# Query and key projections of the prompt rows as three fp32r products of split weights and split x, and the convolution state loaded later

## What is computed

```python
q, k, v, z, xbc, dt = jnp.split(x @ w_in, IN_SPLITS, axis=-1)
q = _rope(q.reshape(b, L, 2 * ATT_HEADS, ATT_QK_DIM), pos)
k = _rope(k.reshape(b, L, 2 * ATT_HEADS, ATT_QK_DIM), pos)
...
xbc_pad = jnp.concatenate([conv_prev.astype(xbc.dtype), xbc], axis=1)
conv = conv_b + sum(xbc_pad[:, i:i + L] * conv_w[i] for i in range(CONV_WIDTH))
```

## Time and profile before

| | us |
|---|---|
| median of 3 runs | 1794.18 |
| lowest, highest | 1792.43, 1798.73 |
| profiled execution, span | 1790.7 |

### The profile page before, as it was taken

One profiled execution on the slowest core, in us unless ns is written; L12 is line 12 of the kernel. 1 busy time (PEld: TensorE's weight loads), 2 busy tenths in 40 slices (PEclk: granted clock), 3 DMA queues, 4 the chain that ended last, 5 costly groups with the idle time before them and its releaser, 6 DMA issues.

```text
span 1790.7 us, 23663 instructions
## 1 busy us (share of the span) xinstructions
PE 1743.2 (97%) x8760; PEld 1362.3 (76%) x8760; DVE 1214.5 (68%) x1659; ACT 845.4 (47%) x898; POOL 111.8 (6%) x120
## 2 busy tenths in 40 slices
PE   7999999999999999999999999999999999999998
PEld 4646487689999574558677888888888888888886
DVE  2687635255544287552715989899898989898994
ACT  1122211144442122212204777777777777777774
POOL 0630000000000252000001000000000000000000
PEclk9999999999999999999998999999999999999999
DMA  9556554855424445663672989899998989898980
GB/s 321 189 201 213 217 188 153 287 171 188 166 94 178 156 162 199 218 229 135 242 258 72 349 298 381 335 380 338 372 394 315 392 318 387 320 384 336 379 321 26
DMA packets 218514, 459.32 MB, mean 257 GB/s; under 512 B 10878, under 2 KB 49976, under 8 KB 218422
## 3 DMA queue, kind: packets, MB, share of 16 engines
q1 hardware_dynamic: 212710, 442.63, 68.3%
q0 software_dynamic: 3424, 11.50, 2.0%
q10 hardware_dynamic: 2304, 4.20, 0.6%
HBM read 444.97 MB, written 13.46 MB: 256 GB/s over the span
## 4 chain that ended last, share of the span: by engine, by line
PE 85%; DVE 7%; ACT 4%; issue 1%; DMA 1%; SPq 1%; POOL 0%; ACTq 0%; DVEq 0%; POOLq 0%
PE bank L1228 83%; PE bank L1232 3%; DVE arena L2701 1%; DVE ring_low L2170 1%; ACT high L1784 1%; DMA out<-mem_rows 1%; DVE R L2315 1%; ACT L1784 1%; ACT arena L1855 0%; POOL arena L972 0%; ACT ye_high L1823 0%; ACT SQ L1876 0%; DVE st L2673 0%; DVE st L2594 0%; SPq L734 0%
## 5 line engine op out<-in xcount | busy, mean ns | idle before, releaser
L2170 DVE TENSOR_TENSOR ring_low<-ring,high 128x2048 fp32r<-128x2048 f32 x264 | 598.7, 2288 | 81.3 <-ACT high L1784 80.5
L1784 ACT ACTIVATE high<-ring 128x2048 fp32r<-128x2048 f32 x264 | 505.1, 1918 | 141.8 <-PE bank L1228 137.6
L1228 PE MATMUL bank<-high,xg_high 128*128 128x512 f32 x704 | 278.1, 395 | 7.3 <-DVE ring_low L2170 7.0
L1228 PE MATMUL bank<-ring_low,xg_high 128*128 128x512 f32 x704 | 274.6, 390 | 0.0
L1228 PE MATMUL bank<-high,xg_low 128*128 128x512 f32 x704 | 274.2, 389 | 0.0
L1228 PEld LDWEIGHTS bank<-high,xg_high 128*128 128x128 f32 x704 | 132.2, 188 | 34.7 <-DVE ring_low L2170 8.4
L1228 PEld LDWEIGHTS bank<-ring_low,xg_high 128*128 128x128 f32 x704 | 132.2, 188 | 28.0
L1228 PEld LDWEIGHTS bank<-high,xg_low 128*128 128x128 f32 x704 | 132.3, 188 | 25.7
L1855 ACT ACTIVATE arena<-bank 128x512 f32<-128x512 f32 (+3 forms) x95 | 46.3, 525 | 217.1 <-PE bank L1228 141.5
L1228 PE MATMUL bank<-high,he_high 128*128 128x512 f32 x352 | 140.0, 398 | 0.0
L1228 PE MATMUL bank<-ring_low,he_high 128*128 128x512 f32 x352 | 137.4, 390 | 0.0
(11 more groups left out here) (327 smaller groups left out, 2578.0 us busy)
## 6 DMA issues: line engine op xcount, KB each, us to landing
ring<-in_w_exp_gu SPq DMA_DIRECT2D x176, 1024.0 KB, 9.9
ring<-in_w_exp_down SPq DMA_DIRECT2D x40, 2048.0 KB, 10.5
ring<-in_w_in SPq DMA_DIRECT2D x12, 2048.0 KB, 11.2
ring<-in_w_ffn_gu SPq DMA_DIRECT2D x22, 1024.0 KB, 8.7
ring<-in_w_ckv SPq DMA_DIRECT2D x8, 2048.0 KB, 9.1
ring<-in_cache_mem_k SPq DMA_DIRECT2D x16, 1024.0 KB, 8.1
ring<-in_cache_mem_v SPq DMA_DIRECT2D x16, 1024.0 KB, 6.6
ring<-in_cache_attn_k SPq DMA_DIRECT2D x32, 256.0 KB, 3.9
```

The costliest lines, as they stand in the source:

```text
L1228: return M.matmul(out, lhsT, rhs, start=start, stop=stop)
L1784: S.activation(high_bufs[h % HIGH_BUFS][:], ring[:, s, j * HALF:(j + 1) * HALF], ACT.Copy).then_inc(split_high, 1)
L2170: V.tensor_tensor(ring_low[:, s, part], ring[:, s, part], high_bufs[h % HIGH_BUFS][:], ALU.subtract).then_inc(split_low, 1)
```

## The change

The q and k products of the prompt rows (t = 0 and 1) are no longer fp32 products of `xT` and `ring`. They become three fp32r products for each of the eight chunks: `xq_high` by high weights, `xq_low` by high weights, `xq_high` by low weights.

- ACT writes `xq_high` (8 x 128 x 264, in SQ's memory) and the two high halves of the weight (`tok_high0`, `tok_high1`, 128 x 2048 each, in the arena's memory). For layer 0 this stands between the copies of `memT` and the setup exponentials; for layer 1 the high halves of q stand at the head of the norm that ends layer 0, and `xq_high` at its end. The high halves of k follow the dt steps.
- DVE writes `xq_low` (8 x 128 x 264, in R's memory) and the low halves into the ring's own slot (`ring_low`): those of q after dt, those of k after `other_quarters` of k.
- PE takes both prompt tiles together: first all products with the high halves, then the low ones (`prompt_rows`).
- SQ's memory was that of `sc_in`. The load of the old convolution state is now on POOL behind the rope of the decode rows and a wait until k is done on PE, and `scT` is between rounds m = 2 and m = 3.
- The split of decode q has memory of its own (`pair_q`); the clearing of `pair_in` goes from the layer's start to behind the last taps.

```diff
+            def tok_high_part(l, c, j):
+                s, n = rg.arrived(act, (l, c)), tok_half(l, c, j)
+                if c == "k":
+                    act.wait_ge(tok_high_used, n - 1)
+                    act.wait_ge(tok_low, n - 1)
+                S.activation(tok_high_bufs[j][:], ring[:, s, j * HALF:(j + 1) * HALF], ACT.Copy).then_inc(tok_high, 1)
...
             def norm(l, i):
+                if (l, i) == (0, 2):
+                    passed(act, (0, "d", 7))
+                    for j in range(2):
+                        tok_high_part(1, "q", j)
...
+                def prompt_rows(c):
+                    s = rg.arrived(pe, (l, c))
+                    low = ring_low[:, s, :].rearrange("p (k n) -> p k n", k=KT)
+                    bks = [turns.open(pe, (l, "tok", c, t)) for t in range(2)]
+                    for j in range(2):
+                        pe.wait_ge(tok_high, tok_half(l, c, j) + 1)
+                        high = tok_high_bufs[j].rearrange("p (k n) -> p k n", k=4)
+                        for t in range(2):
+                            for kk in range(4):
+                                ...
+                                mm(bks[t][:], xq_high[:, k, t * P:(t + 1) * P], high[:, kk, :], k == 0, False)
+                            for kk in range(4):
+                                ...
+                                last = mm(bks[t][:], xq_low[:, k, t * P:(t + 1) * P], high[:, kk, :], False, False)
+                        last.then_inc(tok_high_used, 1)
+                    for t in range(2):
+                        for k in range(KT):
+                            if t == 0 and k % 4 == 0:
+                                pe.wait_ge(tok_low, tok_half(l, c, k // 4) + 1)
+                            last = mm(bks[t][:], xq_high[:, k, t * P:(t + 1) * P], low[:, k, :], False, k == KT - 1)
+                        full(last)
...
+                def tok_low_part(c, j):
+                    s, n = rg.pos[(l, c)] % RING, tok_half(l, c, j)
+                    part = slice(j * HALF, (j + 1) * HALF)
+                    passed(dve, (l, "tok", c, 2))
+                    dve.wait_ge(tok_high, n + 1)
+                    V.tensor_tensor(ring_low[:, s, part], ring[:, s, part], tok_high_bufs[j][:], ALU.subtract
+                                    ).then_inc(tok_low, 1)
...
                 V.tensor_tensor(da, dtv, An[:, l, :], ALU.mult).then_inc(da_ready.sem, 1)
+                for j in range(2):
+                    tok_low_part("q", j)
                 other_quarters(1, "k", qk_raw[0:8, 2, 512:1024])
+                for j in range(2):
+                    tok_low_part("k", j)
...
-                if l:
-                    passed(pool, (l - 1, "var", 2))
-                pool.dma_start(sc_in, a["state_conv"][l].rearrange("b i n -> (b i) n")
-                               ).then_inc(conv_state_landed, 16)
...
                     rope_ready.wait(pool, l, i)
+                    if i == 0:
+                        passed(pool, (l, "tok", "k", 1))
+                        pool.dma_start(sc_in, a["state_conv"][l].rearrange("b i n -> (b i) n")
+                                       ).then_inc(conv_state_landed, 16)
```

More of the change, by code:

```diff
@@ L204, in psum_groups @@
         add("V", "acs")
-        add("V", "scT")
         for m in range(8):
@@ L1402, in _ @@
                 full(last)
[L1403 to L1407, removed]
                 for b in range(8):
@@ L1414, in _ @@
                         pair_ready.wait(pe, l)
-                    full(on_all(bk, b, pair_in))
+                    full(on_all(bk, b, pair_q))
+                    if b == 2:
+                        bk = turns.open(pe, (l, "scT"))
+                        pe.wait_ge(conv_state_landed, 16 * (l + 1))
+                        for m in range(8):
+                            last = tr(bk[:, 24 * m:24 * m + 24], sc_in[:, m * P:(m + 1) * P], 24)
+                        full(last)
                     if b == 0:
@@ L1892, in norm @@
                                  ).then_inc(xT_act.sem, 1)
+                if (l, i) == (0, 2):
+                    for k in range(KT):
+                        scaled.wait(act, l, 8 * i + k)
+                        S.activation(xq_high[:, k, :], R[:, k, :], ACT.Identity, bias=col_b(l, i, k)
+                                     ).then_inc(xq_high_ready.sem, 1)
             S.preload_act_table_set(EXP_AND_LN)
@@ L1898, in _ @@
                          lambda bk: bk[:].rearrange("p (k n) -> p k n", k=4))
+            copied(act, ("xin", 4))
+            for k in range(KT):
+                S.activation(xq_high[:, k, :], xT[:, k, :], ACT.Copy).then_inc(xq_high_ready.sem, 1)
+            for j in range(2):
+                tok_high_part(0, "q", j)
             act.wait_ge(small_landed, 16 * 9)
@@ L2355, in _ @@
             decode_columns(0)
+            for k in range(KT):
+                xq_high_ready.wait(dve, 0, k)
+                V.tensor_tensor(xq_low[:, k, :], xT[:, k, :], xq_high[:, k, :], ALU.subtract
+                                ).then_inc(xq_low_ready.sem, 1)
             dve.wait_ge(small_landed, 16 * 9)
@@ L2461, in _ @@
                         later_taps(m - 1)
+                    if m == 2:
+                        bk = take(dve, (l, "scT"))
+                        emptied_after((l, "scT"), V.tensor_copy(
+                            win[:, :, 0:3, :], bk[:, 0:192].rearrange("p (m b i) -> p m i b", m=8, b=8)))
                 later_taps(7)
+                step.inc(V.memset(pair_in[0:40].bitcast(F32), 0.0))
                 dve.wait_ge(dve_steps, step.n)
```

52 lines of the change are left out of this document (36 added, 16 removed).

## The result

The changed kernel takes 1799.8 us (median of 19 runs, 1794.1 to 1803.4) beside 1794.7 us for the kernel before on the same chip (19 runs). The ratio of the two over all runs is 1.002, 95% interval 1.001 to 1.0029: 3.6 us more (the medians alone are 5.1 us apart). The loss is small, though the interval lies wholly above 1, and the time lies above the predicted range. The products gained what was predicted and more; nothing of it arrived. Its profiled execution has a span of 1796.8 us.

The account below looks back on a forecast made before the run. PE was taken to bound the kernel, with the chain of waits on it for 85% of the span. Gains of 2.2 us (layer 0) and 3.9 us (layer 1), 6.1 in sum, gave span 1784.6, median 1788.1 us, range 1784.3 to 1794.

Parts of the forecast that it names:

- what was predicted: PE's q and k products: gains of 1.5 us (q) and 3.7 us (k) in layer 0, 5.0 us in layer 1.

Follow-up runs that it names:

- e8: The changed kernel with POOL's DMA of the convolution state after its second row tile instead of its first; ratio 1.0005 against the kernel before.
- e7: The changed kernel with POOL waiting in each row tile for its first rotary operation to end before the second; ratio 1.0001 against the kernel before.
- e4: The kernel before with three clearings of tmp on DVE ahead of the split of decode q, adding idle time on PE; ratio 1.0085.
- e12: The changed kernel with a memset on DVE between the two operations of the split of decode q; ratio 1.0028 against the kernel before.
- e2: The changed kernel with POOL waiting for the split of decode q before the moved DMA and the prompt rope; ratio 0.9997 against the kernel before.
- e5: The changed kernel with the q half of the decode rows roped and split as soon as it is there; 1786.0 us, ratio 0.9945 against the kernel before.

## What to carry to other kernels

When the bounding engine is made faster, list for its next wait every chain that ends there, and move each with the event that starts it: PE had waited 0.3 us at `qb` before, and 1.4 us would have been left even with the old split. When TensorE gets a new wait of a microsecond or more, reckon with a stretch at half clock behind it, which is no certainty: at `qb`, waits of 1.4 to 4.1 us lost 1.7 to 3.4 us more here (1.37 us of waiting 1.7, and 2.11 us already 3.4), while two of 1.4 and 1.6 us at `sST` lost nothing more. Try first to take the awaited operation out of the busy place altogether: one reordering was worth 13.5 us here. A step that is moved "out of the way" on POOL may stand in DVE's way instead.

## What the runs showed of the hardware that I had not expected

- Waits of TensorE at `qb` and what followed: 0.3 and 0.5 us, full clock; 1.37 us, about 3.4 us at half clock (e8, a clock of 0.75 over 59.8 to 66.6 us); 2.11 us (e7), 3.2 us (the changed kernel) and 4.1 us (e4), 6.8 us at half clock. With products in the gap the clock stayed at 1.00.
- The length of the wait does not settle it alone. In e12 a wait of 3.19 us in layer 0 was followed by some 3.4 us at half clock and one of 3.15 us in layer 1 by 6.8; at `sST` waits of 1.56 and 1.41 us (e8) were followed by none, one of 3.11 us (e2) by 6.8. What decides between them stays open.
- POOL's DMA right ahead of two operations with no wait between them: a small operation of DVE waited for both, 3.48 us where alone it takes 0.68.
- Two subtractions of DVE in a row held POOL's operation for 5.39 us in place of 1.25; in e5 POOL got in between two of the same kind (2.77 and 2.66 us for turns of 0.72). What decides that stays open.
